# A two-layer decoder trunk on one core: expert stages reordered, the first layer's expert results scattered to rows of their own and summed in the next input projection

## The reference, cut to what matters

```python
for layer in range(2):
    hn = rms_norm(h, norm_mix[layer])
    h = h + (even_mixer if layer == 0 else odd_mixer)(hn, ...)   # in-projection, attention, out-projection
    h = h + hier_moe(rms_norm(h, norm_ffn[layer]), ...)
...
def hier_moe(h, ...):          # T = 2048 tokens, 32 experts, 2 experts for each token
    eid, gate = ...            # top group, then the top two experts in it
    # (token, expert) pairs, ordered by expert, each expert's rows padded to whole blocks of 128
    hid = silu(xb @ w_gate[e]) * (xb @ w_up[e])     # xb: 128 x 1024, FF = 256
    out = hid @ w_down[e]
    y = segment_sum(out * gate, token)              # 2 rows of out for each token
```

## Time and profile before

| | |
|---|---|
| median of 3 runs | 3131.38 us (3124.84 to 3132.12) |
| the profiled execution | 3119.75 us, its span 3117.8 us, granted clock 0.936 |
| PE busy | 2673.4 us (86%) |
| DVE, ACT, POOL busy | 1747.1, 1260.4, 724.0 us |
| DMA | 509.57 MB, mean 163 GB/s |
| experts of layer 0 | from 1198 to 1720 us, first to last expert matmul |
| input projection of layer 1 | from 1738 to 2010 us |
| experts of layer 1 | from 2598 to 3100 us |

### The profile page before, as it was taken

One profiled execution on the slowest core, in us unless ns is written; L12 is line 12 of the kernel. 1 busy time (PEld: TensorE's weight loads), 2 busy tenths in 40 slices (PEclk: granted clock), 3 DMA queues, 4 the chain that ended last, 5 costly groups with the idle time before them and its releaser, 6 DMA issues. The chain is left out here.

```text
span 3117.8 us, 48627 instructions
## 1 busy us (share of the span) xinstructions
PE 2673.4 (86%) x15109; PEld 2236.8 (72%) x15112; DVE 1747.1 (56%) x3154; ACT 1260.4 (40%) x2369; POOL 724.0 (23%) x923
## 2 busy tenths in 40 slices
PE   5999979997968947998898599799879947989997
PEld 4999958875847836777676488578658836767775
DVE  4222246665755665667765366588733354676664
ACT  3222132225841104556654222288611104675653
POOL 1000023321110002444343143211100002444433
PEclk9999989998988968999999799899979968999998
DMA  6111112215536516899997322222154415999995
GB/s 243 50 56 52 40 60 78 75 65 165 163 121 234 194 61 216 261 301 302 316 281 228 118 87 80 91 83 88 53 198 143 149 39 179 298 359 285 283 308 132
DMA packets 175389, 509.57 MB, mean 163 GB/s; under 512 B 53800, under 2 KB 81456, under 8 KB 150320
## 3 DMA queue, kind: packets, MB, share of 16 engines
q1 hardware_dynamic: 142480, 393.69, 34.7%
q0 software_dynamic: 32800, 114.51, 15.4%
HBM read 374.56 MB, written 133.56 MB: 163 GB/s over the span
## 5 line engine op out<-in xcount | busy, mean ns | idle before, releaser
L1700 DVE TENSOR_TENSOR moe_parts<-expert_w,moe_parts 128x1024 fp32r<-128x1024 f32 x384 | 452.3, 1221 | 238.4 <-ACT moe_parts L1649 234.9
L1582 PE MATMUL ps<-moe_parts,moe_xT 128*128 128x512 f32 x2232 | 551.6, 403 | 23.0 <-issue 16.0
L1582 PEld LDWEIGHTS ps<-moe_parts,moe_xT 128*128 128x128 f32 x2232 | 418.1, 191 | 125.3 <-issue 20.5
L1649 ACT ACTIVATE moe_parts<-expert_w 128x1024 fp32r<-128x1024 f32 x384 | 373.3, 1047 | 80.3 <-PEq L155 78.8
L1109 PE MATMUL ps<-out_w,out_catT 128*128 128x512 f32 x1344 | 322.4, 399 | 14.2 <-DVE out_w L1265 11.8
L560 PE MATMUL ps<-in_gate_w,in_gate_hnT 128*128 128x384 f32 (+1 forms) x1536 | 319.4, 367 | 7.4 <-DVE in_gate_w L679 7.4
L1582 PE MATMUL ps<-moe_parts,moe_hidT 128*128 128x512 f32 x1116 | 289.0, 408 | 26.9 <-DVE moe_hidT L1713 24.2
L560 PEld LDWEIGHTS ps<-in_gate_w,in_gate_hnT 128*128 128x128 f32 x1536 | 278.7, 190 | 37.4 <-issue 7.5
L1109 PEld LDWEIGHTS ps<-out_w,out_catT 128*128 128x128 f32 x1344 | 255.7, 192 | 69.4 <-DVE out_w L1265 12.6
L560 PE MATMUL ps<-in_qk_w,in_qk_hnT 128*128 128x512 f32 x1152 | 268.4, 394 | 9.2 <-DVE in_qk_w L679 9.2
L1582 PEld LDWEIGHTS ps<-moe_parts,moe_hidT 128*128 128x128 f32 x1116 | 205.7, 191 | 76.2 <-DVE moe_hidT L1713 32.8
(11 more groups left out here) (262 smaller groups left out, 4150.8 us busy)
## 6 DMA issues: line engine op xcount, KB each, us to landing
expert_w<-in_w_gate SPq DMA_DIRECT2D x64, 1024.0 KB
expert_w<-in_w_up SPq DMA_DIRECT2D x64, 1024.0 KB
expert_w<-in_w_down SPq DMA_DIRECT2D x64, 1024.0 KB
hn_d<-out_hn SPq DMA_DIRECT2D x32, 512.0 KB, 2.6
in_gate_xt<-in_x SPq DMA_DIRECT2D x16, 512.0 KB
in_qk_xt<-in_x SPq DMA_DIRECT2D x16, 512.0 KB
att_k<-k_d SPq DMA_DIRECT2D x64, 128.0 KB, 2.9
out_ht<-in_x SPq DMA_DIRECT2D x16, 512.0 KB, 4.6
```

Of the source, the lines that this page charges most:

```text
L1582: last = nc.tensor.matmul(out, left[:, a, k, :], right(b, k), start=(n == 0 and k == 0), stop=(n == 2 and k == K_ - 1))
L1649: nc.scalar.activation(parts[:, j, 0, at], K.expert_w[:, j, at], ACT.Copy).then_inc(w_high.sem, 1)
L1700: nc.vector.tensor_tensor(parts[:, j, 1, at], K.expert_w[:, j, at], parts[:, j, 0, at].bitcast(F32), ALU.subtract).then_inc(w_low.sem, 1)
```

## The change

Three things change together.

1. In the experts' stage, the pieces of the weight split are placed differently among the work on the blocks, the down pieces of an expert are split one expert later (in its own first block), SP loads gate/up and down parts by separate counts, PE starts raise with the two products of x's high part and waits for the low part only ahead of the third (and likewise in lower), and ACT reads the gate from the table, which takes POOL's copy away (L1542).
2. Indirect transfers get bounds: rows past the end are not to be moved. `who` of an empty row is now past the end of `hn_d` (in both layers). xg is cleared once at the start.
3. In layer 0, the scatter doesn't add: each (token, choice) pair has a row of its own in a new tensor `y_d` (4096 rows), written plainly; empty rows are out of bounds. The sum h + y1 + y2 is made in the input projection of layer 1: SP loads three tiles instead of one to `terms` (which lies in out_w, so the load of layer 1's output weights moves into the attention phase), DVE adds them into xt (`add_terms`), and SP stores the sum to h_d; `norm`, which overwrites xt, waits for that store. In layer 1 the scatter still adds.

```diff
@@ Kernel.build @@
+            self.y_d = self.dram("y_d", [2 * T, D])
@@ project_in @@
             def load(s):
...
+                if not isinstance(n, int) or n >= 2:
+                    alone(sp, summed, n - 1, K.tick_sp)
+                for r, src in enumerate((K.h_d[0], K.y_d[0:T], K.y_d[T:2 * T])):
+                    sp.dma_start(terms[:, j, r, :], rows(src, n)).then_inc(x_in[j], 16)
+
+            def store_sum(s):
+                alone(sp, summed, s.n + 1, K.tick_sp)
+                sp.dma_start(rows(K.h_d[0], s.n), xt[:, s.slot(2), :]).then_inc(sum_st[s.slot(2)], 16)
...
             def step(s):
                 if s.plus(2).within(NT):
                     load(s.plus(2))
+                if not even and s.plus(1).within(NT):
+                    store_sum(s.plus(1))
...
+            def add_terms(s):
+                j = s.slot(2)
+                v_.wait_ge(x_in[j], s.turn(2) * 48 + 48)
+                until(v_, turned, s.n - 1)
+                own_.link(nc.vector.tensor_tensor(xt[:, j, :], terms[:, j, 0, :], terms[:, j, 1, :], ALU.add))
+                nc.vector.tensor_tensor(xt[:, j, :], xt[:, j, :], terms[:, j, 2, :], ALU.add).then_inc(summed.sem, 1)
+
             def norm(s):
                 j = s.slot(2)
                 until(v_, rms_x, s.n + 1)
+                if not even:
+                    v_.wait_ge(sum_st[j], s.turn(2) * 16 + 16)
...
+                if not even and s.plus(2).within(NT):
+                    add_terms(s.plus(2))
@@ experts @@
                 nc.gpsimd.indirect_dma_start(xg[:, :], None, K.hn_d[layer],
-                                             bass.IndirectOffsetOnAxis(ap=who[:, :], axis=0)).then_inc(gathered_s, 16)
+                                             bass.IndirectOffsetOnAxis(ap=who[:, :], axis=0),
+                                             bounds_check=T - 1, oob_is_err=False).then_inc(gathered_s, 16)
...
+                if layer == 0:
+                    g.indirect_dma_start(K.y_d, bass.IndirectOffsetOnAxis(ap=where[:, :], axis=0), y[:, :], None,
+                                         bounds_check=2 * T - 1, oob_is_err=False).then_inc(scattered_s, 16)
+                else:
+                    g.indirect_dma_start(K.out, bass.IndirectOffsetOnAxis(ap=where[:, :], axis=0), y[:, :], None,
+                                         compute_op=ALU.add).then_inc(scattered_s, 16)
+            g.memset(xg[:, :], 0.0).then_inc(cleared, 1)
...
+                until(pe, x_high, m + 1)
                 until(pe, hid_done, m)
+                product(gup, xT, lambda h, k: wgu[:, h, k, :, :], DK, ((0, 0), (0, 1)))
+                until(pe, x_low, m + 1)
+                product(gup, xT, lambda h, k: wgu[:, h, k, :, :], DK, ((1, 0),)).then_inc(up.sem, 1)
...
@@ on ScalarE @@
             def first_block(i, j, m, behind, ahead):
                 ni, nj = i + j, 1 - j
+                if behind:
+                    act(m - 1)
                 if ahead:
-                    a.wait_ge(K.expert_in[layer][nj], ni * 48 + 48)
-                    if behind:
-                        until(a, up, m)
-                    split(ni, nj, range(GU_PIECES))
-                act(m)
-                x_out(m + 1)
+                    a.wait_ge(K.up_in[layer][nj], ni * 32 + 32)
+                    split_up(nj, (0,))
+                x_out(m)
+                if ahead:
+                    split_up(nj, (1,))
                 if behind:
-                    y_scaled(m - 1)
+                    y_scaled(m - 2)
+                split_down(i, j)
                 if ahead:
-                    split(ni, nj, range(GU_PIECES, PIECES))
+                    split_up(nj, range(2, GU_PIECES))
```

More of the change, by code:

```diff
@@ L446, in square @@
                 j = s.slot(2)
[L447 removed]
+                if even:
+                    a.wait_ge(x_in[j], s.turn(2) * 16 + 16)
+                else:
+                    until(a, summed, s.n + 1)
                 until(a, rms_x, s.n - 1)
@@ L1720, in first_block @@
                 ni, nj = i + j, 1 - j
+                if behind:
+                    hidden(m - 1)
                 if ahead:
-                    split(ni, nj, range(GU_PIECES // 2))
+                    split_up(ni, nj, (0,))
+                x_out(m)
                 if behind:
```

229 lines of the change are left out of this document (132 added, 97 removed).

## The result

| | before | changed |
|---|---|---|
| median | 3128.1 us (3122.2 to 3132.1, 4 runs) | 3171.9 us (3167.5 to 3173.8, 4 runs) |
| profiled execution, its span | 3119.75, 3117.8 us | 3167.47, 3165.6 us |

The change made the kernel slower: ratio 1.0149, 95% interval 1.0132 to 1.0167. 3171.9 us lie outside the range of the prediction.

The account below looks back on a forecast made before the run. It took PE's work plus PE's waits to bound each stage. Its terms, -46 - 14 + 2 + 43 + 3 = -12 us on the profiled 3119.75, gave 3107.8, or 3119 us as median against 3131.4; range 3080 to 3155.

Parts of the forecast that it names:

- -12 -6 -6 in layer 0 and -9 -8 in layer 1: Experts: us off hidden-row waits (12, 9), their slow clock (6, layer 0 only), low parts and other waits with stage start (6, 8).
- part 2: Expert stages: bounds on indirect transfers and layer 0's plain scatter shorten gathers and relieve the DMA engines.
- The gather's 9.62 should fall to about 8.5 there: Layer 0 experts: time from one turn's end to the next, through the gather, falls from 9.62 to about 8.5 us.
- 23 of 27.7 us for layer 0: Layer 0 experts: PE's waits for gathered rows, 27.7 us, lose 23, including the 8.9 ahead of the last lower.
- by 3 us: Layer 1 experts: with the other waits gone, the gather's waits grow by 3 us, as the add stays.
- the gather stays the bound: Rival, expert stages: turn to turn from about 9.2 us on, removed waits return at the gather; +23, 3154 us; chance 0.23.
- The last block's gather, 8.9 us: End of layer 0's experts: this wait, for a block that doesn't exist, goes, as no row is left to move.
- The input projection, +43: Layer 1's input projection: a new loop through SP's sum store makes a tile 18.3 us against 14.8; +43 us.
- 5.2 + 7.3 + 1.28 + 4.5 = 18.3: Projection loop, us: rotated heads to SP's load, three loads and store landed (bounds 6.5 and 9.5), norm, norm_rotate.
- the first rival: Projection: sum store isn't held by loads, landing 2.9 us after issue; +7 instead of +43, 3083 us; chance 0.17.
- The start of the projection, +3: Projection's first norm, delayed by tile 0's sum: two more loads, two passes, one store; +3 us (0 to 6).
- -46 -14 +2 +43 +3 = -12: Sum in us: layer 0 experts, layer 1 experts, clearing xg for both layers, projection loop, projection start.

Follow-up runs that it names:

- light_order: New expert order and split weight loads alone on the kernel before, weights' loads after the first two experts cut to a sixteenth: 3007.6 us, ratio 0.9634; layer 0 441.6.
- light_w: Changed kernel with the weights' loads after the first two experts cut to a sixteenth (wrong results): 3070.5 us, ratio 0.9826; layer 0 441.3.
- gate_early: Changed kernel with SyncE issuing the gate weights' load ahead of the down weights, spreading an expert's loads: 3148.7 us, ratio 1.0094 to the kernel before.
- sum_first: Changed kernel with SyncE issuing the store of a tile's sum ahead of the three next loads: 3113.9 us, ratio 0.9983 to the kernel before.
- best_start: Changed kernel with two gather buffers, sum store ahead of the loads, second tile's addition behind first tile's norm and low part: 3067.3 us, ratio 0.9811 to before.
- no_oob: Changed kernel without bounds on gathers and plain scatter; empty rows gathered from a valid row, scattered to spare rows: 3196.1 us, ratio 1.0232 to before.
- two_xg: Changed kernel with two buffers for gathered rows, used in turn: 3129.2 us, ratio 1.0026 to the kernel before.

## Why the prediction was wrong

**The order in the experts, -12 -6 -6 in layer 0 and -9 -8 in layer 1: right in mechanism, lost in the sum.** The waits for hidden rows and low parts are gone from the list. light_order shows that with quick gathers this is worth even more than foretold (67 us against 24 in layer 0). But the prediction took these gains and the gather's separately.

**The step that failed is in part 2: "The gather's 9.62 should fall to about 8.5 there ... I take 23 of 27.7 us for layer 0", and for layer 1 that the gather's waits grow "by 3 us".** For the gathers that PE waits for, turn to turn came to 10.7 us in layer 0 and 11.6 in layer 1 (2.5 to the issue, 8.3 or 9.0 to the rows); counted from the end of a turn, as the 9.62 is, that is 9.6 and 10.4. PE's waits for rows went up by 4 and 32 us. That is the rival "the gather stays the bound", whose threshold of 9.2 us was passed; I had given it 0.23. The 9.62 was itself one of the shorter rounds: the medians before, counted in the same way, are 9.9 and 10.2. Another part of the error was to read the gather's length as a matter of its own bytes and of the share of the whole stage. It depends on what is in flight at its issue. The prediction said nothing of when the weights' loads go out, though the new code ties them to split pieces that now stand closer together. light_w shows that the weights' traffic makes the gather long enough to be waited for, gate_early that their timing is part of it (0.4 us of a gather). By the medians the gather's round hardly changed, so most of the added waiting is PE coming to the turn sooner; as they hold only gathers that were waited for, this is an estimate and not shown. The section "Queues, rings and completion order" of the Trainium skill's page "DMA: Bandwidth & Descriptors" says that each DMA engine takes turns between the queues that have work. By that rule the gather, in the software queue, would get slower beside a full hardware queue without standing behind it; the 8.3 to 9.5 us beside 3 MB of weights fit this, but no run here tells sharing from standing behind.

The last block's gather, 8.9 us, vanished as said. The idle time of layer 0, first to last turn, is -8.9 for it, +12.9 for the other gathers and some -20.5 for the waits that the order removed. PE's busy time fell by 15.7 us where 6 were foretold.

**The bounds** are worth some 25 us in the new order and nothing in the old one, where the waits for hidden rows rose (24.2 to 49.4) as those for rows fell. **The plain scatter** is worth 21 to 27 and 8.5. Both would have been well sized only after asking which loop they shorten.

**The input projection, +43: right mechanism, a term too small.** The loop was foretold at 5.2 + 7.3 + 1.28 + 4.5 = 18.3. It measured 4.85 (1866.87 to 1871.72) + 8.48 (to 1880.20) + 1.2 + 4.4 = 18.9 in this tile, 19.4 on average, over 14.7 for PE's tile. The term mis-sized is the three loads and the store, 7.3 against 8.5, inside its bounds of 6.5 and 9.5. Eleven tiles at 4.7, and 3.4 and 1.6 at the ends, make +57. That the store isn't held, the first rival, is refuted by sum_first.

**The start of the projection, +3: it took +11.6.** The mark also holds the end of the experts, where two plain scatters run beside the input weights (ScalarE waited 9.3 us there, 7.08 in the earlier trace rows); up to SyncE's first load it is only 1.2 us longer. From that load to the first turn it took 19.4 us (1707.9 to 1727.3) against 9.0: the sum store stands behind loads here too, and the second tile's terms are added first. best_start shows that moving the addition alone gives nothing.

**The sign.** -46 -14 +2 +43 +3 = -12 became -21 for layer 0 with its tail, +6 for layer 1, +6 for the marks ahead of the two expert stages and +57: +48. Of the 60 us between, some 34 are lost in the expert stages, where the gather is the bound (-46 became -32, -14 became +6), 14 in the projection, 9 at its start and 4 in the rest.

## What to carry to other kernels

A wait that is removed pays only up to the next loop's length, so write down the period of every loop that goes round with a block (here the splits, the gather through its one buffer, and the scatter), and see which is next. In this kernel a transfer's time depended on what was issued in the few microseconds ahead of it (a store 6.95 or 3.0 us, a gather 9.0 or 8.7): list the issues around it in the new order before you price it, and in one queue put the transfer that something waits for first. Two moved lines were worth 52 us here.

## What was unexpected of the hardware

- Skipped rows move no data but still have packets: in the software queue the changed kernel has 32864 packets with 89.37 MB, no_oob 32864 with 114.51. Of all packets 6144 more are under 512 bytes (60760 against 54616), which is just the number of rows that are skipped (1920 and 1792 of the gathers, 512 of the two gathers past the end of each layer, 1920 of the scatter).
- A small operation of GpSimd (L527, 128x18) took 1.32 us when it started beside VectorE's norm of 128x1024 and 0.22 when it ran ahead of it. The same shows on a copy of 128x1 in other places (0.18 against 1.18).
- In layer 1 of the changed kernel eight of the sixteen waits for rows of 1.86 us or more were followed by a slow `lower` (PE's product with the down weights), as here 4.58 us against 3.01 elsewhere; after shorter waits none was. In the 4.55 us from 2934.65 the granted clock was 0.62, against 1.00 in the 5 us up to 2933 and in the 2.8 us behind, so PE ran at 1.2 GHz for part of them. The matmuls of `lower` from 2642 to 3144 us took 425 ns each, those of two_xg in layer 1 408. The granted clock of that stretch is 0.97 against 0.99 in the earlier trace rows.

```profile
2933.73 1.16 PE L1645 MATMUL ps<-ident,moe_xg 128*128 128x128 f32 x8 [2.43 <-DMA moe_xg<-hn_d,moe_who]
2934.65 4.58 PE L1637 MATMUL ps<-moe_parts,moe_hidT 128*128 128x512 f32 x12
```
